# Neighbourhood attention beside the gate projections: where TensorE takes a pair's score matmuls

## The reference, cut to what matters

```
s_nb  = einsum('brqhd,brikhd->bhrqik', grid(q_rot), k_band) * scale + bias   # masked outside the window
s_ctx = einsum('brqhd,bchd->bhrqc', grid(q), k_ctx) * scale
p     = softmax(concat([s_nb, s_ctx]))
o     = einsum(p_nb, v_band) + einsum(p_ctx, v_ctx)
```

## Time and profile before

| | |
|---|---|
| median of 3 runs | 1553.56 us (1553.02 to 1554.49) |
| the profiled execution's own time | 1553.23 us |
| its span | 1551.4 us |
| TensorE busy | 1500.2 us, 97% of the span |
| VectorE, ScalarE, POOL busy | 66%, 45%, 27% |
| the stage of the change | 904.2 to 1048.1 us of the span |
| TensorE's wait inside it | 0.8 us once on VectorE, 1.1 us twice on ScalarE |

### The profile page before, as it was taken

How to read it: one execution, slowest core, us unless ns; L and a number is a source line. 1 busy time by engine, 2 the same in 40 slices (tenths; PEclk the granted TensorE clock), 3 DMA queues, 4 the chain that set the end, 5 groups by cost and what they waited for, 6 DMA issues and landing times. The chain is left out here.

```text
span 1551.4 us, 20959 instructions
## 1 busy us (share of the span) xinstructions
PE 1500.2 (97%) x8416; PEld 1278.5 (82%) x8416; DVE 1030.1 (66%) x1555; ACT 690.8 (45%) x1025; POOL 423.6 (27%) x363
## 2 busy tenths in 40 slices
PE   6999998998999999999999999998999999999997
PEld 5778886787888888888988877776878999999886
DVE  7676456759678865768652654448855899995335
ACT  6644346755533344323533344443446544543232
POOL 0024315631611210000170022214432466650002
PEclk9999999999999999999999999999999999999999
DMA  8342112363344432675433422314462122224211
GB/s 312 109 150 95 63 55 96 129 221 121 114 150 176 163 109 108 218 276 212 148 109 118 133 96 95 126 50 161 153 227 109 52 107 106 101 101 161 90 73 55
DMA packets 50987, 203.61 MB, mean 131 GB/s; under 512 B 18528, under 2 KB 18784, under 8 KB 32138
## 3 DMA queue, kind: packets, MB, share of 16 engines
q1 hardware_dynamic: 37346, 172.04, 30.9%
q0 software_dynamic: 8576, 28.29, 5.0%
q10 hardware_dynamic: 4968, 1.94, 0.5%
HBM read 181.24 MB, written 21.00 MB: 130 GB/s over the span
## 5 line engine op out<-in xcount | busy, mean ns | idle before, releaser
L587 PE MATMUL ps<-xl,whi 128*128 128x512 f32 (+1 forms) x1136 | 393.2, 346 | 0.0
L1889 DVE TENSOR_TENSOR wlo<-raw,whi 128x2048 fp32r<-128x2048 f32 x89 | 217.0, 2438 | 156.3 <-ACT whi L1236 156.1
L1236 ACT ACTIVATE whi<-raw 128x512 fp32r<-128x512 f32 (+1 forms) x191 | 232.4, 1223 | 130.3 <-PE ps L588 83.8
L586 PE MATMUL ps<-xh,whi 128*128 128x256 f32 (+1 forms) x768 | 263.0, 342 | 6.2 <-DVE xl L1933 6.2
L588 PE MATMUL ps<-xh,wlo 128*128 128x256 f32 (+1 forms) x768 | 257.0, 335 | 0.0
L587 PEld LDWEIGHTS ps<-xl,whi 128*128 128x128 f32 x1136 | 216.4, 190 | 24.3
L586 PEld LDWEIGHTS ps<-xh,whi 128*128 128x128 f32 x768 | 146.9, 191 | 30.7 <-issue 18.1
L588 PEld LDWEIGHTS ps<-xh,wlo 128*128 128x128 f32 x768 | 146.8, 191 | 14.8
L586 PE MATMUL ps<-xhr,whi 128*128 128x512 f32 (+1 forms) x368 | 136.8, 372 | 2.4 <-DVE xl L1933 2.4
L588 PE MATMUL ps<-xhr,wlo 128*128 128x512 f32 (+1 forms) x368 | 136.4, 371 | 0.0
L2327 DVE SCALAR_TENSOR_TENSOR xr<-ps,pc,xr 128x511 f32<-128x511 f32 x88 | 65.3, 747 | 37.1 <-ACT xr L1236 35.6
(11 more groups left out here) (467 smaller groups left out, 3615.4 us busy)
## 6 DMA issues: line engine op xcount, KB each, us to landing
raw<-in_w_in SPq DMA_DIRECT2D x35, 1024.0 KB, 5.0
raw<-in_ffn_w SPq DMA_DIRECT2D x33, 1024.0 KB, 4.8
raw<-in_ada SPq DMA_DIRECT2D x24, 1024.0 KB, 4.8
raw<-in_w_up SPq DMA_DIRECT2D x22, 1024.0 KB, 4.8
raw<-in_w_down SPq DMA_DIRECT2D x11, 1024.0 KB, 4.8
xd<-X POOLq DMA_DIRECT2D x8, 512.0 KB, 5.5
td<-vr POOLq DMA_DIRECT2D x16, 256.0 KB, 3.0
raw<-td SPq DMA_DIRECT2D x4, 1024.0 KB, 4.7
```

The costliest lines, as they stand in the source:

```text
L586: pe.e.matmul(o, lh, rh, start=start, stop=False)
L587: pe.e.matmul(o, lh, rl, start=False, stop=False)
L1236: m = ac.e.activation(dst, src, func, **more)
L1889: up(ve.e.tensor_tensor(lo, raw[conv_at[j] % 3][:, :], hi.bitcast(F32), ALU.subtract), "wlo")
```

## The change

The block that takes the two banks and issues a pair's eight score matmuls is moved within the loop of TensorE's program. For an even i it now stands after D(i) and T(i-2), directly ahead of G(i/2-2). The order of TensorE becomes, for even i: D(i), T(i-2), S(i, i+1), G(i/2-2); for odd i, as before: D(i), T(i-2). No other engine's program is changed, no instruction is added or removed. The order in which scores and transposes draw banks from their pool changes with it.

```
             use[0] = "scores"
             for i in range(35):
                 if i < 32:
-                    if i % 2 == 0:
-                        ht, t = i // 8, item(i)[1]
-                        bs = [take(("as", 32 + i + o), "at_s", 32 + i + o + 1) for o in range(2)]
-                        for o, b in enumerate(bs):
-                            r = slice(64 * o, 64 * o + 64)
-                            keys = kr2[r, ht, :].rearrange("p (r c) -> p r c", c=64)[:, :, KC0[t]:KC0[t] + 32]
-                            pe.e.matmul(b[:, 0:256].rearrange("p (r c) -> p r c", c=32), qt[r, ht, P * t:P * t + P],
-                                        keys, start=True, stop=True)
-                        for o, b in enumerate(bs):
-                            r = slice(64 * o, 64 * o + 64)
-                            done(pe.e.matmul(b[:, 256:512], qn[r, ht, P * t:P * t + P], kc[r, ht, :],
-                                             start=True, stop=True), ("as", 32 + i + o))
                     gate_half(i)
                 if 0 <= i - 2 < 32:
                     weigh(32 + i - 2, pq2[(i - 2) % 4], 4, "at_o")
+                if i < 32 and i % 2 == 0:
+                    ht, t = i // 8, item(i)[1]
+                    bs = [take(("as", 32 + i + o), "at_s", 32 + i + o + 1) for o in range(2)]
...
                 if i >= 4 and i % 2 == 0:
                     pe.wait_ge(sig["vt"], 128)
                     gather_pair(i // 2 - 2)
```

More of the change, by code:

```diff
@@ L1055, in tensor_program @@
                     weigh(32 + i - 2, pq2[(i - 2) % 4], 4, "at_o")
+                if i < 32 and i % 2 == 0:
+                    ht, t = i // 8, item(i)[1]
+                    bs = [take(("as", 32 + i + o), "at_s", 32 + i + o + 1) for o in range(2)]
+                    for o, b in enumerate(bs):
+                        r = slice(64 * o, 64 * o + 64)
+                        keys = kr2[r, ht, :].rearrange("p (r c) -> p r c", c=64)[:, :, KC0[t]:KC0[t] + 32]
+                        pe.e.matmul(b[:, 0:256].rearrange("p (r c) -> p r c", c=32), qt[r, ht, P * t:P * t + P],
+                                    keys, start=True, stop=True)
+                    for o, b in enumerate(bs):
+                        r = slice(64 * o, 64 * o + 64)
+                        done(pe.e.matmul(b[:, 256:512], qn[r, ht, P * t:P * t + P], kc[r, ht, :],
+                                         start=True, stop=True), ("as", 32 + i + o))
                 if i >= 4 and i % 2 == 0:
```

## The result

The changed kernel took 1557.98 us (median of 12 runs, 1555.89 to 1562.21); the kernel before, run beside it on the same chip, took 1554.24 (12 runs, 1553.02 to 1555.86). The ratio is 1.0021, with a 95% interval of 1.0013 to 1.003: slower by 3.3 us, between 2.0 and 4.7. The profiled execution's own time was 1557.28 us.

The account below looks back on a forecast made before the run. TensorE was taken to bound the stage. Start +1.05, seven waiting pairs +1.9 and six free pairs -1.0 make +1.9 us, 1555.5 against the median 1553.56; range 1553.1 to 1557.4, holding 8 in 10.

Parts of the forecast that it names:

- The steps inside the stage: TensorE's pairs inside the stage: seven at +0.27 us make +1.9, six at -0.17 make -1.0.
- a free pair: Undisturbed pair of TensorE steps in the stage, three changes of form instead of four: 8.70 us, a gain of 0.17.
- a pair with the wait: Pair where D(i+2) waits about 0.44 us for ScalarE's gate tile copy behind the high parts: 9.14 us, 0.27 longer.
- rivals A (copy in time): ScalarE's gate copy is in time, only the drain saving counts: -1.2 us, 1552.4, down to 1547.8; chance 10%.
- B (S dearer): Going from half rows straight to half columns makes S 1.45 us or more: +5.0 at 1.5, 1558.6; chance 12%.
- The start: At the first transposes, T(0)'s wait grows from 0.8 to some 2 us with S(2, 3) behind it: D(5) +1.05.
- I take it that what the stage gains or loses reaches the end undiminished: From this stage to the kernel's end: TensorE's last gathers release the next stage, so the whole +1.9 us arrives.
- Rival C: After the stage, VectorE or a DMA is late for another reason, so the lag doesn't reach the end: 1553.6; chance 8%.
- The rule and the row: Saving one change of form on TensorE: 0.17 us by the trace row, 0.05 by the skill's drain rule (sum +2.6).

## Why the prediction was wrong

**The steps inside the stage held.** S ahead of G 1.06 (forecast 1.06), T to D 0.35 (0.38), a free pair 8.66 (8.70), a pair with the wait 9.12 and 9.22 (9.14), seven waits on `tm`. D(5) to the next stage +0.80; by the forecast's own terms +1.9 - 1.05 = +0.85. No T waited for its scaling. The rivals A (copy in time) and B (S dearer) are refuted by the `tm` waits and by the 1.06.

**The start held, as far as waits go.** T(0) waited 2.13 ("some 2 us") and came at 915.54 (915.8); +1.08 in both repeats, for a forecast +1.05.

**What failed is the step "I take it that what the stage gains or loses reaches the end undiminished", taken as the whole of the path to the end.** TensorE's own loss did arrive, as said there. What was put at nothing is a second path: VectorE's first product in the next stage waits for the landing of the last gate store, which the forecast held for hidden because the store's distance from S doesn't grow. Its issue did keep to that (10.9 us after S(30) before, 7.5 after), and the landing was late even so. In the profile of before the wait was hidden by 0.6 us (the store landed at 1045.83 + 5.3 = 1051.1, the product started at 1051.70). Every other profile of the old order has it open, and the new order's lags are longer by 0.5 us on the mean, 1.73 in the pair first compared, of which about half reaches the end. Rival C took the same step from the other side, that the loss might not arrive; nothing in the range stood for its growing.

**A second term put at nothing is the clock behind the longer wait.** The sum took S(2, 3) at 1.06 there. The clock fell behind the wait in one of the five profiles that have it at 2.13 (the changed kernel three times, the one with the later load, the one with the short store), S(2, 3) took 1.99, and in all it cost 1.6 us there, 0.3 on the mean of the five.

**The sizes add up only in part.** Start +1.08, inside +0.80 and half of a lag of +0.5 make +2.1 us, with the clock +2.4. The three measurements are +3.3, +3.3 and +2.5 (1.0021, 1.0021 and 1.0016 of 1554 us), with intervals that all hold +2.4 as well, so up to 0.9 us stays unexplained. The granted clock of whole executions, which every run gives as a mean, doesn't settle it. Against the kernel before, run beside it, it is lower by 0.0012 and 0.0006 in the repeats and by 0.0010 with the later load (standard errors 0.0005 to 0.0007), and one fall of the kind seen, 3.4 us at half speed in 1555, is worth 0.0011. But it is lower by 0.0007 and 0.0010 too where that wait was filled or was gone. So the new order may well meet more falls, and if it does, they don't hang on that wait alone.

**The base and the spread.** The forecast was counted from 1553.56, the median of three runs; twelve gave 1554.24. So of the 2.5 us by which 1557.98 missed 1555.5, 0.7 is the base, and 1.8 is the change as the medians give it (+3.7 against +1.9). The 0.7 us allowed for the runs' spread was too little: the kernel before has medians of 1554.24, 1554.57, 1554.84 and 1555.08 in four sets of runs, and single runs of the changed one span 6 us. Had the range allowed for the 1.5 us between the highest of these and 1553.56, its upper end would have been 1558.9.

**The rule and the row.** A free pair gained 0.21 us (8.66 over 13 pairs against 8.87), where the row of before gave 0.17. The Trainium skill, "TensorE: Matmul & The Clock Gate", step-by-step part, by its drain of about 128 columns (an estimate of 0.05 us at full clock), would have given a quarter of it: the trace doesn't agree, and the row was the better price for a change of form. The same page, "Single matmul latency", gives 166 ns at full clock as the constant part of a matmul that stands alone; that is nearer to the 0.21, and the page doesn't speak of a change of form there.

## What to carry to other kernels

When a step of TensorE is moved nearer to the one that reuses its bank, look up what stands ahead of the releasing copy on the other engine: here a 1.90 us conversion ahead of a 0.6 us copy turned a gain of 2.7 us into a loss of 0.8, and putting the conversion behind the copy got it back. Don't move work behind a wait that is already known: here it cost 1.1 us. At the border of a stage, list the waits that the program has and the profile doesn't show, and read how much covers each, from more than one execution.

## What the runs showed of the hardware

After an idle time of 2.13 us the granted clock fell to the lower level in one of five executions, and after 3.27 us in the one profiled; in the other four at 2.13 it stayed up. The stores of 256 KB ahead of the spectra's loads landed 2.3 and 3.5 us after their issue in the kernel before, and one issued 0.85 us ahead of these loads in the changed kernel after 2.3; the last one, issued some 2.4 us after six loads of 256 KB with a load of 1 MB behind them, took 5.3 to 7.3 us over 15 executions. With that 1 MB moved later it took 5.4 and 5.5. In three executions of the kernel before it was 5.3, 6.2 and 6.4. A change between full and half forms of TensorE's matmuls is worth 0.21 us here (four in a pair against three), and going from half rows to half columns costs no more than from half rows to the full array: 1.06 us for S in both.
